# Gate pieces of the modulation summed per partition on VectorE, the FFN's gate inside the first down pass

## The reference, cut to what matters

```python
mod = (silu(cond) @ ada_w + ada_b).reshape(B, 6, 1, 1024)
sh1, sc1, gt1, sh2, sc2, gt2 = [mod[:, i] for i in range(6)]
h = rms_norm(x, norm_g[0]) * (1 + sc1) + sh1
y, st = mixer_sublayer(h, ...)          # q,k,v,o, gates, gMLP, pool, conv, then w_out
x = x + gt1 * rms_norm(y, norm_g[1])
h = rms_norm(x, norm_g[2]) * (1 + sc2) + sh2
a = dwconv_centred(h @ ffn_up, ffn_conv)
val, gate = split(a, 2)
x = x + gt2 * rms_norm((silu(gate) * val) @ ffn_down, norm_g[3])
```

## Time and profile before

| | before |
|---|---|
| median of 3 runs | 899.6 us (899.44 to 901.97) |
| profiled execution, span | 899.8 us |
| PE busy | 848.5 us, 94% |
| DVE busy | 527.6 us, 59% |
| ACT busy | 355.3 us, 39% |
| loads moved | 104.25 MB, mean 116 GB/s |
| matmuls of up loop and w_in tiles (L1476) | 48.0% of the chain that ended last |
| matmuls of out and down projection (L1663) | 21.1% of it |
| gate matmuls (L1432) | 2.5% of it |

### The profile page before, as it was taken

How to read it: one execution, slowest core, us unless ns; L and a number is a source line. 1 busy time by engine, 2 the same in 40 slices (tenths; PEclk the granted TensorE clock), 3 DMA queues, 4 the chain that set the end, 5 groups by cost and what they waited for, 6 DMA issues and landing times.

```text
span 899.8 us, 13256 instructions
## 1 busy us (share of the span) xinstructions
PE 848.5 (94%) x5011; PEld 749.2 (83%) x5011; DVE 527.6 (59%) x763; ACT 355.3 (39%) x564; POOL 69.8 (8%) x92
## 2 busy tenths in 40 slices
PE   3779989999999999989999999999999999999996
PEld 1569978988986768766999999999999967888785
DVE  2872283677575584679565555655556565434854
ACT  3782332222221143567344342443424443334642
POOL 2650000000000002621000000000000000000000
PEclk9779997999999899999999999999999999999998
DMA  9863113243322158435322213222232144333562
GB/s 291 277 180 91 50 54 89 92 79 116 96 71 89 53 187 262 159 107 171 110 71 70 83 56 93 70 70 81 59 93 70 47 148 156 118 121 113 191 204 96
DMA packets 98063, 104.25 MB, mean 116 GB/s; under 512 B 6407, under 2 KB 79271, under 8 KB 97767
## 3 DMA queue, kind: packets, MB, share of 16 engines
q1 hardware_dynamic: 94103, 95.77, 35.0%
q0 software_dynamic: 2064, 6.23, 2.4%
q10 hardware_dynamic: 1856, 1.71, 0.6%
HBM read 100.94 MB, written 2.75 MB: 115 GB/s over the span
## 4 chain that ended last, share of the span: by engine, by line
PE 84%; DVE 6%; DMA 4%; ACT 3%; issue 2%; SPq 1%; DVEq 0%; ACTq 0%
PE PAIR L1476 48%; PE PAIR L1663 21%; DMA RAW<-in_ada_w_dram 3%; PE PAIR L1432 3%; PE PAIR L1447 2%; PE PAIR L1486 2%; PE PAIR L1625 2%; PE PAIR L1620 2%; DVE WLO L977 1%; PE PAIR L1603 1%; ACT WHI L734 1%; PE PAIR L1586 1%; PE PAIR L1592 1%; PE PAIR L1634 1%; PE PAIR L1457 1%
## 5 line engine op out<-in xcount | busy, mean ns | idle before, releaser
L1476 PE MATMUL PAIR<-Hhi,WHI 128*128 128x320 f32 x960 | 226.1, 314 | 8.2 <-DVE SA L1138 3.8
L1476 PE MATMUL PAIR<-Hlo,WHI 128*128 128x320 f32 x960 | 224.0, 312 | 0.0
L1476 PE MATMUL PAIR<-Hhi,WLO 128*128 128x320 f32 x960 | 223.7, 312 | 0.0
L977 DVE TENSOR_TENSOR WLO<-RAW,WHI 128x1024 fp32r<-128x1024 f32 (+1 forms) x115 | 142.0, 1243 | 56.9 <-ACT WHI L734 56.1
L1476 PEld LDWEIGHTS PAIR<-Hhi,WHI 128*128 128x128 f32 x960 | 163.3, 191 | 10.5 <-issue 6.3
L1476 PEld LDWEIGHTS PAIR<-Hlo,WHI 128*128 128x128 f32 x960 | 163.7, 191 | 0.0
L1476 PEld LDWEIGHTS PAIR<-Hhi,WLO 128*128 128x128 f32 x960 | 163.3, 190 | 0.0
L734 ACT ACTIVATE WHI<-RAW 128x1024 fp32r<-128x1024 f32 (+1 forms) x115 | 119.3, 1049 | 34.7 <-DMA RAW<-in_ada_w_dram 14.4
L1663 PE MATMUL PAIR<-WHI,ASHI 128*128 128x512 f32 x300 | 94.9, 398 | 5.1 <-DVE ASLO L1301 4.0
L1663 PE MATMUL PAIR<-WHI,ASLO 128*128 128x512 f32 x300 | 94.9, 398 | 0.0
L1663 PE MATMUL PAIR<-WLO,ASHI 128*128 128x512 f32 x300 | 94.7, 397 | 0.0
(11 more groups left out here) (211 smaller groups left out, 876.1 us busy)
## 6 DMA issues: line engine op xcount, KB each, us to landing
RAW<-in_ada_w_dram SPq DMA_DIRECT2D x48, 512.0 KB, 4.2
RAW<-in_ffn_up_dram SPq DMA_DIRECT2D x44, 512.0 KB, 3.8
RAW<-in_ffn_down_dram SPq DMA_DIRECT2D x44, 512.0 KB, 3.7
RAW<-in_w_in_dram SPq DMA_DIRECT2D x20, 512.0 KB, 5.0
RAW<-in_w_out_dram SPq DMA_DIRECT2D x16, 512.0 KB, 4.8
out_dram<-X SPq DMA_DIRECT2D x5, 512.0 KB, 5.5
X<-in_x_sample_dram POOLq DMA_DIRECT2D x4, 512.0 KB, 7.9
XSA<-in_x_sample_dram ACTq DMA_DIRECT2D x2, 512.0 KB, 7.3
```

The lines of the kernel that those rows point to most:

```text
L977: dve.tensor_tensor(WLO[:, u % RING, 0:w], RAW[:, u % RING, 0:w], WHI[:, u % RING, 0:w].bitcast(F32), ALU.subtract).then_inc(lo_split, 1)
L1476: last = pe.matmul(t[:, 512 * half:512 * half + HALF], w[:, n_or_slot, cols(k)], h[:, k, HALF * half:HALF * half + HALF], start=(k == 0 an ...
```

## The change

The step `ada` goes, with its matmuls, its MODROW copies and its four PSUM uses. In its place stand single-unit steps `ga` p q (piece p, unit q of four). DVE takes the raw unit itself: for each of its two row chunks and both groups it multiplies the 128x512 block by the condition's column and adds it to GATE, four instructions for a unit (the two first of a piece are a plain multiplication), each counted on the semaphore `gate_sum`. The slot of a raw unit comes free when its fourth sum is done. The step `p2` then adds the partitions with one matmul of 512 columns for each group against a matrix of ones, and DVE goes on with bias and norm weight as before.

The pieces also move. The four units of piece 4 now stand one after each of q0, q1, k0 and k1; those of piece 5 stand around gv (two before the step gv1, two after it), ahead of mx0. In code the unit list of that stretch is q0, ga40, q1, ga41, k0, ga42, k1, ga43, vg0, vg1, gv0, gv1, ga50, ga51, ga52, ga53, gu0, then the two units of the modulation block ad 4. p2 4 stays between B8 and C8; p2 5 moves from after pl1 to between B9 and C9. Pieces 10 and 11 both go into pass A of the down projection: eight `ga` steps, one before each of the chunks 3 to 10, p2 10 after chunk 10 and p2 11 after chunk 12. The first three units behind the up loop, which were raw, are now the down chunks 0 to 2, split inside the loop.

```diff
-    ("q", 0), ("q", 1), ("k", 0), ("k", 1), ("v", 0), ("v", 1), ("v", 2), ("kt", 0), ("kt", 1), ("gi", 0), ("gf", 0),
-    ("gv", 0), ("gv", 1), ("mx", 0), ("mx", 1), ("gu", 0), ("ct", 0),
+    ("q", 0), ("ga", 4, 0), ("q", 1), ("ga", 4, 1), ("k", 0), ("ga", 4, 2), ("k", 1), ("ga", 4, 3), ("v", 0), ("v", 1), ("v", 2), ("kt", 0), ("kt", 1), ("gi", 0), ("gf", 0),
+    ("gv", 0), ("ga", 5, 0), ("ga", 5, 1), ("gv", 1), ("ga", 5, 2), ("ga", 5, 3), ("mx", 0), ("mx", 1), ("gu", 0), ("ct", 0),
...
-    ("ada", 4), ("B", 8), ("p2", 4), ("C", 8), ("pz", 1), ("pl", 0), ("B", 9), ("ada", 5), ("C", 9), ("o", 0),
-    ("pl", 1), ("p2", 5), ("o", 1)]
+    ("B", 8), ("p2", 4), ("C", 8), ("pz", 1), ("pl", 0), ("B", 9), ("p2", 5), ("C", 9), ("o", 0), ("pl", 1), ("o", 1)]
...
-            + [("lo", 1), ("epi", 3), ("epi", 4), ("nrm", 3), ("nrm", 4), ("tr", 2), ("hi", 2), ("ada", 10), ("tr", 3),
-               ("hi", 3), ("lo", 2), ("tr", 4), ("hi", 4), ("lo", 3), ("lo", 4), ("p2", 10)])
+            + [("lo", 1), ("epi", 3), ("epi", 4), ("nrm", 3), ("nrm", 4), ("tr", 2), ("hi", 2), ("tr", 3),
+               ("hi", 3), ("lo", 2), ("tr", 4), ("hi", 4), ("lo", 3), ("lo", 4)])
...
-PLAN_DOWN = ([("ada", 11)] + A_DOWN[0:2] + [("p2", 11)] + A_DOWN[2:] + [("epi", 0)]
+GATE_DOWN = [("ga", 10 + n // 4, n % 4) for n in range(8)]
+PLAN_DOWN = (A_DOWN[0:3] + [x for n in range(8) for x in (GATE_DOWN[n], A_DOWN[n + 3])] + [("p2", 10)] + A_DOWN[11:13]
+             + [("p2", 11)] + A_DOWN[13:] + [("epi", 0)]
...
-            if s[0] in ("ada", "ad"):
+            if s[0] == "ga":
+                n_gate += 1
+                release[pos] = (gate_sum, 4 * n_gate, at_)
+            elif s[0] == "ad":
...
+            def gate_part(p, q, u):
+
+                dve.wait_ge(raw_in[u % RING], raw_count(u))
+                c0 = 512 * (p % 2)
+                for k in range(2):
+                    for group in range(2):
+                        total, w = GATE[:, group, c0:c0 + 512], COND[:, 2 * q + k, 2 * group:2 * group + 1]
+                        part = RAW[:, u % RING, 512 * k:512 * k + 512]
+                        if q == 0 and k == 0:
+                            ins = dve.tensor_scalar(total, part, w, None, ALU.mult)
+                        else:
+                            dve.wait_ge(gate_sum, n_part[0] - 1)
+                            ins = dve.scalar_tensor_tensor(out=total, in0=part, scalar=w, in1=total,
+                                                           op0=ALU.mult, op1=ALU.add)
+                        ins.then_inc(gate_sum, 1)
+                        n_part[0] += 1
 
...
-            def ada(key, first):
-
-                t = wait_free(pe, key)
-                for q in range(4):
-                    u = first + q
-                    pe.wait_ge(raw_in[u % RING], raw_count(u))
-                    for k in range(2):
-                        last = pe.matmul(t[0:4, 0:512], COND[:, 2 * q + k, :], RAW[:, u % RING, 512 * k:512 * k + 512],
-                                         start=(q == 0 and k == 0), stop=(q == 3 and k == 1))
-                    last.then_inc(ada_used if q < 3 else filled[USE[key][0]], 1)
...
-            def piece2(key, row_key):
-
-                wait_copied(pe, row_key)
+            def piece2(key, p):
+
+                pe.wait_ge(gate_sum, 16 * ((4, 5, 10, 11).index(p) + 1))
                 t = wait_free(pe, key)
+                c0 = 512 * (p % 2)
                 for group in range(2):
-                    last = pe.matmul(t[:, 512 * group:512 * group + 512], SELHL[:, group, :], MODROW[:, :],
+                    last = pe.matmul(t[:, 512 * group:512 * group + 512], ONES[:, :], GATE[:, group, c0:c0 + 512],
                                      start=True, stop=True)
                 last.then_inc(filled[USE[key][0]], 1)
 
```

More of the change, by code:

```diff
@@ L111, in plan_units @@
     for s in PLAN:
-        if s[0] == "ada":
-            units += [("ada", s[1], q) for q in range(4)]
+        if s[0] == "ga":
+            units.append(s)
         elif s[0] == "ad":
@@ L135, in plan_units @@
             units += [("down", n) for n in k_chunks(s)]
-        elif s[0] == "ada":
-            units += [("ada", s[1], q) for q in range(4)]
+        elif s[0] == "ga":
+            units.append(s)
         upto[("down",) + s] = len(units)
@@ L174, in plan_pairs @@
                     use((stage, "epi", g), PASS_PAIR[stage][g], 1)
-            elif s[0] in ("tr", "ada", "p2"):
+            elif s[0] in ("tr", "p2"):
                 use((stage,) + s, OUT_PAIR[(stage,) + s], readers.get(s[0], 1))
@@ L400, in raw_unit @@
         def raw_unit(n):
-            return UNITS[n][0] == "ada"
+            return UNITS[n][0] == "ga"
+        assert not any(raw_unit(UP0 + 2 * FT + n) for n in range(AHEAD))
         def is_split(n):
-            return not raw_unit(n) or 0 <= n - UP0 - 2 * FT < AHEAD
+            return not raw_unit(n)
         splits_to = [sum(is_split(m) for m in range(n)) for n in range(NU + 1)]
@@ L458, in hybrid_trunk_layer @@
             n = UPTO[key]
-            if stage and s[0] not in ("k", "k2") and key != ("down", "ada", 11):
+            if stage and s[0] not in ("k", "k2"):
                 goal[at_] = goal[at_ - 1]
@@ L509, in source @@
             def source(u):
-                if u[0] == "ada":
+                if u[0] == "ga":
                     _, p, q = u
@@ L746, in mix @@
             def mix(s):
-                kind, n = s
+                kind, n = s[0], s[1]
                 if kind == "xs":
@@ L1079, in mix @@
             def mix(s):
-                kind, n = s
-                if kind == "ada":
-                    ada(s, n)
+                kind, n = s[0], s[1]
+                if kind == "ga":
+                    gate_part(s[1], s[2], UPTO[s] - 1)
                 elif kind == "ad":
@@ L1374, in _ @@
                         .then_inc(n_lo, 1)
-                elif s[0] == "ada":
-                    ada(("out",) + s, s[1])
-                elif s[0] == "p2":
-                    piece2(("out",) + s, s[1])
             base, per = n_link[0], 2 * RING
             split_base = splits_to[UP0 + AHEAD]
+            split_to(UP0 + AHEAD)
             with dve.Fori(0, LOOPS) as i:
@@ L1406, in _ @@
             split[0] += 2 * FT
-            split_to(UP0 + 2 * FT + 5)
+            split_to(UP0 + 2 * FT + AHEAD)
             for at_, s in enumerate(PLAN_DOWN, UP_STEP + 1):
-                if s == ("ada", 11):
-                    chunks_to(2 * KC + 3)
-                elif s[0] in ("k", "k2"):
+                if s[0] in ("k", "k2"):
                     chunks_to(chunk_limit("down", s))
                 split_to(goal[at_])
-                if s[0] == "ada":
-                    ada(("down",) + s, s[1])
+                if s[0] == "ga":
+                    gate_part(s[1], s[2], UPTO[("down",) + s] - 1)
                 elif s[0] == "p2":
@@ L1692, in _ @@
                     last.then_inc(filled[USE[key][0]], 1)
-                elif s[0] == "ada":
-                    ada(("out",) + s, UPTO[("out",) + s] - 4)
-                elif s[0] == "p2":
-                    piece2(("out",) + s, ("out", "ada", s[1]))
             for half in range(2):
@@ L1720, in _ @@
                     chunks("down", s)
-                elif s[0] == "ada":
-                    ada(("down",) + s, UPTO[("down",) + s] - 4)
                 elif s[0] == "p2":
-                    piece2(("down",) + s, ("down", "ada", s[1]))
+                    piece2(("down",) + s, s[1])
 _INS = ["x_prompt", "x_sample", "state_C", "state_n", "state_m", "c", "c_ctx", "norm_g", "ada_w", "ada_b", "w_in",
```

33 lines of the change are left out of this document (14 added, 19 removed).

## The result

The changed kernel takes 943.7 us (median of four, 938.0 to 946.1) against 900.5 us before: ratio 1.0455, interval 1.0421 to 1.0489. The forecast of 940 us with 922 to 954 holds, and so does its sign. The profiled execution spans 942.1 us against 899.8, 42.3 us more. Of the chain that ended last PE holds 72% now (84% in the earlier trace rows), DVE 11%, loads 7%.

What follows compares the result with a forecast made beforehand. PE work was taken to bound the kernel (84% of the chain). Terms 11.4 + 2.6 + 25.9 - 3.9 - 0.9 + 5.6 = +40.7 on 899.8 gave 940 us, range 922 to 954, own bounds about 928 to 952.

Steps and rivals of the forecast that it cites:

- Part 1: q to v: load, split and sum run serially through the ring; PE waits 11.4 us before v, plus 2.6 clock.
- part 2: ga50 to mx0: the same serial loop on the DVE chain delays PE's gu0 by 25.9 us (21 to 30).
- The wheel's terms: In the ring loop of load, split, sum: pair of loads 5.3 us, split 2.4, four sums 2.6, a turn of 10.3.
- The pair's 5.3: In the ring: two loads issued 0.4 us apart land after 5.3 us, with 4.5 and 6.1 as ends.
- Part 3: Mixers without ada 4 and ada 5: C8 -3.8, p2 5 -1.9, clock +1.8, sum -3.9 us (-9 to -2).
- Part 4: Output stage without ada 10: DVE chain -1.9, clock +1.0, sum -0.9 us (-2 to +1).
- Part 5: Down pass: first chunk -1.4, clock +2.6, two p2 +1.9, stalls +2.5, sum +5.6 us (0 to +12).
- the three stalls: Pass A of the down projection: the ring's loop stalls PE at three of eight places, +2.5 us.
- The hidden loop: Rival: load, split and sum fit behind PE's tile; -9 at the mixers, -1.9 at the output; 889 us, chance 0.10.
- v is not held: Rival in q to v: loads land early and sums overlap, so v starts almost on time; 926 us, chance 0.10.
- pass A held at every turn: Rival in the down pass: pairs land after 6.1 us, all eight stall by 1.5; 950 us, chance 0.13.

Runs made afterwards that it cites:

- buffers of their own: Changed kernel with the mixers' eight gate units loaded into four separate buffers, no splitting ahead at a sum, piece 5's sums ahead of the scans: 904.0 us.
- the fill there: Changed kernel plus 20 unused matmuls of 128 by 512 in PE's idle time between p2 5 and C9: 936.4 us.
- the buffers: Changed kernel with only the down pass's eight gate units taken out of the ring, loaded by POOL into two separate buffers: 939.0 us.
- the rule: Changed kernel where a ga step no longer lets units ahead be split, so DVE takes a unit's sum before a later unit's split: 922.2 us.
- every second chunk: Changed kernel with the down pass's eight sums spread to one per two chunks rather than one per chunk: 948.6 us.
- the FFN gate alone: Kernel before with only ada 10 and ada 11 moved off PE, their eight units summed on DVE in the first down pass: 907.8 us.
- thin sums: Changed kernel with the sums' multiply-and-add on 16 of 512 columns, the rest of each sum left out: 928.7 us.

## Why the prediction was right, and where a term was off

**Part 1 and part 2** hold in mechanism and size, and the runs show the mechanism: splitting behind the sum brings v back, and with buffers of their own and piece 5's sums ahead of the scans gu0 comes back too. The wheel's terms were near, with errors that cancel. The pair's 5.3, counted from the end of the sum, was 6.3 in the first turn (74.36 to 80.66, with a small load of constants issued between the two) and 5.4 in the second (85.67 to 91.07); the first sum ended 1.0 us sooner than forecast; a split took 2.4 and the four sums 2.73 instead of 2.6. The prediction took 2.6 against about 2.8 by "VectorE: DVE Perf Modes", section "The DRAIN you can't avoid", of the Trainium skill, by which the next instruction does not start until the pipeline is empty; the section adds that one which isn't held starts earlier. A sum lasts 0.746 us, four of them end to end would be 2.98, and 2.73 was measured, so the instructions overlap somewhat here, as in the earlier trace rows; the figure lies between.

**Part 3** is the term that was mis-sized: -1.9 instead of -3.9. C8 (-4.0) and p2 5 (-1.9) came as worked out. I put +1.8 for the clock behind the two holes, from a stretch of 0.84; behind the 4.9 us before C9 it cost 4.0, as the fill there shows. The nearer row was the 0.50 behind gu0's wait of 3.8 us, in the same group. The other hole, 3.1 us ahead of C8, cost nothing more, and that was luck: C8 ran at the lower level in the kernel before too, with no wait ahead of it:

```profile
294.20:297.00 2.80, 2.80 (x15) 1.79 (x14) 2.58 (x4) 0.00 (x0) 0.00 (x0) 0.56 0.08 29
```

**Part 4** is right in the sum (-1.1, and +0.2 in the up loop, for -0.9). Its terms, -1.9 for the chain and +1.0 for the clock, were not measured apart.

**Part 5** is right in the sum (+5.9 for +5.6), with errors that cancel. The clock cost 1.3 and not 2.6 in this execution, though 2.4 to 2.8 in three others behind the same wait, so 2.6 was not a wrong price; two p2 of 1.72 for one of 1.91 are +1.5 and not +1.9; the three stalls are 3.8 and not 2.5, and they end with WLO as forecast. That leaves 0.7 of the 7.3 unassigned. That the stalls come from the ring is shown by the buffers; that one sum per two chunks would not stall less was not foreseen.

**The rivals.** The hidden loop (889) did not come, and with buffers of its own one sees what it was worth. Then "DMA: Bandwidth & Descriptors", section "Rules for kernel authors", of the Trainium skill applies as it reads: the fixed cost of a load issued early and waited for late overlaps with compute. The trace is in line with it: v waits 0 us instead of 12.5. But that kernel takes 904, not 889. Part 3's clock (+4.0) and the FFN gate (+4.7) are still in it, and DVE's sums ahead of the scans. The rival's -9 at the mixers was also too much: C8 was bound by SS, so two pieces of 6.96 us on PE gave 4.0 and p2 5 1.9. *v is not held* and *pass A held at every turn* did not come; the runs with the rule and with every second chunk are near them in size, for other reasons.

## What to carry to other kernels

A unit that one engine consumes late must not sit in the same in-order ring as the units that feed the bound engine: before moving work, follow one slot from load to release and look whether its release stands behind a later unit's split. Where a matmul is taken out of a stretch that ends with another engine's result, only the part behind that result is won, and the hole that stays can have a price of its own in the granted clock (4.0 us before C9, nothing more at C8). Idle time of an engine (DVE's 2.5 to 4.2 us per step) says that the work fits, not that its data can wait there.

## What the runs showed of the chip that was not expected

- The clock behind a wait. Behind 3.8 us of waiting before gu0 the kernel before ran for some 20 us with stretches at 0.50 (131 to 137 and 145 to 150, with a shorter wait of some 2 us between them, at 141.7), and eight matmuls that nobody reads gave 5.7 us back at the second gu tile, 4.8 in the time.
- It does not follow from the wait alone: with buffers of its own PE waited 5.0 us before gu0, and still the second gu tile came 19.4 us behind gu0 rather than 24.5. The granted clock was 0.61 over 134 to 140 and 1.00 from 145 on. Why is open. Nor is the price the same from one execution to the next: behind the 6.7 us ahead of the down pass the first 5.3 us are at 0.73 to 0.74 in three profiled executions and at 0.50 in five.
- The level also falls where PE has not waited. In the kernel before PE is busy without a hole from 275 on, through ada 4 (6.96 us of matmuls with 4-column weights) and p2 4, at 1.00 up to 294.2; then C8 is at 0.56 and 0.50 up to 301.3. In the runs with the FFN gate alone and with eight matmuls ahead of gu0, where ada 4 also stands, it falls likewise. No run here tells what brings it about.
- One small output transfer on ACT's queue took 7.0 to 7.3 us to issue in four of the fourteen profiled executions (the sum ahead of the split, thin sums, both kernels with buffers of their own and without fills), and at most 2.1 in the other ten; it holds all that ACT has behind it. What holds it was not tried.
